# The projection of dt as one fp32 product in four 32-column groups, with the norm moved behind it

## The chip, the core and the metric

The kernel runs on one core of a Trainium2 chip. The metric is the device time of one execution in microseconds (us). Engines: PE is TensorE (its weight loads are listed apart as PEld), DVE is VectorE, ACT is ScalarE, POOL is GpSimd, SP issues the DMAs.

## The reference

Four layers run in sequence over x of 512 tokens by 1024 features: two of a first kind and two of a second. The change touches the first kind only, in its state-space branch. What matters of it:

```python
h = rmsnorm(x, attn_norm_g[layer])           # x * rsqrt(mean(x*x) + eps) * g
proj = h @ w_in[layer]
gm_u, gm_v, ssm_z, ssm_xbc, ssm_dt, da_q, da_k, da_v, gates = split_cols(proj, IN_SIZES)
...
dt = softplus(ssm_dt + dt_bias)              # ssm_dt: 16 columns of proj, one for each head
```

So `ssm_dt` is a product of h (512 x 1024) with 16 columns of `w_in`. The row factor rsqrt(...) depends on the token alone and the gain g on the feature alone, so that either can be applied before or after the product.

## The kernel before

Everything is fp32. Large products are split: each operand is written as a high part (fp32r) and a remainder, and TensorE makes three fp32r products (hi·hi, hi·lo, lo·hi) of 128 x 128 x 512 each, lines L571 to L573. x lies transposed in `x_t` (128 features by 8 tiles by 512 tokens). `h_hi` and `h_lo` hold the parts of h. Weights come in slabs of 128 x 1024 words into a ring of four (`w_raw`); ACT makes `w_hi` (L561), DVE `w_lo` (L566).

Results leave PE through four banks of PSUM, `pg`, taken in turn: the unit number modulo 4 is the bank. PE may begin a unit only when the bank's previous user has been read out (`bank_free`). In each layer of the first kind the units come in this order: four of `gv` (one for each 128 tokens `tt`), one of `dt`, then twelve of `xbc`, four at a time. With `gv` on banks 0, 1, 2, 3 the `dt` unit has bank 0, and the first four `xbc` units have banks 1, 2, 3, 0 (in the second layer all of this is turned by one bank; I name the banks as in the first). A slab of `xbc` contributes six products to each of the four units.

`gv` is computed on x that has its gain but not yet its norm, while the norm is being formed. Meanwhile DVE makes h (`h_val`, L809) from x, gain and the norm spread over all partitions (in the PSUM bank `spread1`), two tiles after each `gv` slab; ACT rounds it to `h_hi` (L802), POOL and DVE make `h_lo` (L555 and L813). ACT reads the four `gv` units out (L932).

dt: the 16 columns land in `dtw_raw`. ACT writes them twice as high part (L919) and DVE the remainder (L1412), 48 columns in all. PE makes 8 products of `h_hi` with all 48 columns (L2177) and 8 of `h_lo` with the first 16 (L2182), each waiting for its tile of h. They land in rows 0 to 15 and 32 to 47 of the bank. DVE reads the two out (L1430, L1431), which frees the bank, adds the bias (L1436), takes the maximum with 0 (L1437), and goes on with a softplus. All of it is program order on each engine; there is no scheduler.

Of the kernel before, what the change touches and what calls it, by code (L numbers as in the profile page):

```python
# [7 lines left out]
F32 = mybir.dt.float32  # L8
F32R = mybir.dt.float32r
ALU = mybir.AluOpType  # L10
ACT = mybir.ActivationFunctionType
AX = mybir.AxisListType

P = 128
# [4 lines left out]
KD = D // P  # L19
# [5 lines left out]
SSM_I, SSM_H, SSM_P, SSM_N, SSM_G, SSM_K = 1024, 16, 64, 128, 2, 4  # L25
# [6 lines left out]
C_DT = C_XBC + SSM_C  # L32
# [19 lines left out]
BANKS = 4  # L52
LO_DVE = [2, 5, 7]
# [60 lines left out]
def program(nc, t, out, depth=DEPTH, depth2=DEPTH):  # L114
    with ExitStack() as ctx:
# [3 lines left out]
        def over(name, offset, shape, dt):  # L119

            return nc.alloc_sbuf_tensor_at(name, shape, dt, offset=offset)
# [7 lines left out]
        def S(name):  # L129

            if name not in sems:
                sems[name] = ctx.enter_context(nc.semaphore(name))
            return sems[name]
# [6 lines left out]
        x_t = sb("x_t", [P, KD, SEQ])  # L140
# [4 lines left out]
        h_val = sb("h_val", [P, KD, SEQ])  # L145
# [17 lines left out]
        arena_at = next_place()  # L163
# [14 lines left out]
        def at(off, n, shape=None, **kw):  # L178
            a = arena[:, off:off + n]
            return a.rearrange(shape, **kw) if shape else a  # L180
# [5 lines left out]
        pg = ctx.enter_context(nc.psum_tensor("pg", [P, BANKS, SEQ], F32))  # L186
# [11 lines left out]
        dt_b, a_log, a_exp = cut(1), cut(1), cut(1)  # L198
# [49 lines left out]
        dt_t, dt_e, dt_z, dt_p, dt_1 = (at(18432 + 512 * i, 512)[0:SSM_H, :] for i in range(5))  # L248
# [18 lines left out]
        gstat = small[:, 0:8]  # L267
        lstat = small[:, 8:16]

        dtw = over("dtw", arena_at + 4 * 26624, [P, KD, 3 * SSM_H], F32R)  # L270
        dtw_raw = at(26624 + 3 * KD * SSM_H, KD * SSM_H, "p (k n) -> p k n", k=KD)

        m_val = at(0, 4096, "p (i s) -> p i s", i=KD)
        m_lo, m_hi = parts_at("m_lo", 0, KD), parts_at("m_hi", 14336, KD)
# [42 lines left out]
        SL, UN, PM = Schedule(), Schedule(), Schedule()  # L317
# [171 lines left out]
        def gate_unit(i):  # L489
# [5 lines left out]
        SWA_NORM = 3  # L495
        OUT_STEP = [1, 2, 3, 4, 5, 6, 7, 8]

        PER1 = {"par_landed": 16 * 15, "ffn_par_landed": 16 * 3, "dtw_landed": 16, "dtw_hi": 1, "dtw_lo": 1, "dt_done": 1, "h_val": KD, "h_hi_done": KD, "h_lo_dve": len(LO_DVE),
                "h_lo_pool": len(LO_POOL), "dt_x": 1, "dt_exp": 1, "a_exp_ready": 1, "conv_step": 36, "xs_ready": 3, "gv_ready": 1, "gm_rms": 1,
                "gm_vn": TT, "decay_in": 1, "decays": 1, "dt_ready": TT, "ac_split": 1, "gm_wt_ready": 1, "ya_ready": GM_G, "ya_hi_done": GM_G,  # L500
                "ya_split": GM_G, "ac_zeroed": 1, "cb_masked": SSM_G, "seg_bound": SSM_H, "seg_exp": SSM_H, "y_init": KD, "c_exp": SSM_H, "c_scaled": SSM_H, "decay_cb_even": PAIRS, "decay_cb_odd": PAIRS, "y_sq": KD, "y_sq_added": KD - 1, "xw_ready": SSM_G * (TT - 1), "y_gated": KD, "y_rms": 1, "y_inv": 1,
# [13 lines left out]
        def past(name):  # L515

            a, b = min(now[0], depth), max(now[0] - depth, 0)
            return a * PER1.get(name, 0) + b * PER2.get(name, 0)

# [14 lines left out]
        bank_free = [S(f"bank_free{i}") for i in range(BANKS)]  # L534
        pm_ready = S("pm_ready")
        pm_free = [S(f"pm_free{i}") for i in range(4)]

        def pmb(i):
            return pm[:, i % 4, :]
# [35 lines left out]
        def take_bank(pe, u, m, it):  # L575

            wait(pe, bank_free[u % BANKS], count(u // BANKS, m // BANKS, it))
            return pg[:, u % BANKS, :]
# [84 lines left out]
        def pm_left(eng, i):  # L663

            eng.wait_ge(pm_free[i % 4], i // 4 + 1)
# [32 lines left out]
        def gain(k):  # L698
            return g_norm[:, k, :]
# [104 lines left out]
        def norm_dve(dve, k, use, s, first, n, lows=LO_DVE):  # L804

            inv_b = pm_filled(dve, use)
            for i in range(first, first + n):
                dve.wait_ge(slab_done, s + i // 2 + 1)
                nc.vector.scalar_tensor_tensor(h_val[:, i, :], x_t[:, i, :], gain(k)[:, i:i + 1], inv_b, ALU.mult, ALU.mult).then_inc(S("h_val"), 1)  # L809
            for i in range(first + n):  # L810
                if i in lows and (i >= first or lows is not LO_DVE):
                    dve.wait_ge(S("h_hi_done"), past("h_hi_done") + i + 1)
                    nc.vector.tensor_tensor(h_lo[:, i, :], h_val[:, i, :], h_hi[:, i, :].bitcast(F32), ALU.subtract).then_inc(S("h_lo_dve"), 1)  # L813
            if first + n == KD:
                dve.wait_ge(S("h_val"), past("h_val") + KD)
                dve.sem_inc(pm_free[use % 4], 1)

        def norm_pool(pool):
            for i in LO_POOL:
# [3 lines left out]
        def tiles_ready(pe, of):  # L823

            def tile(k):
                for name, tiles in zip((of + "_lo_dve", of + "_lo_pool"), TILES[of]):
                    if k in tiles:
                        pe.wait_ge(S(name), past(name) + tiles.index(k) + 1)
            return tile
# [12 lines left out]
        def unit_left(eng, u, m=0, it=0):  # L842

            wait(eng, bank_free[u % BANKS], count(u // BANKS + 1, m // BANKS, it))
# [21 lines left out]
        def _(act):  # L866
            chain = Chain(act, "act_step")
# [46 lines left out]
            for l in range(depth):  # L914
                enter(l)
                if l > 0:
                    hi_ahead(SL["gv"])
                act.wait_ge(S("dtw_landed"), past("dtw_landed") + 16)
                nc.scalar.activation(dtw[:, :, 0:2 * SSM_H].rearrange("p k (b n) -> p k b n", b=2), dtw_raw.unsqueeze(2).broadcast_to([P, KD, 2, SSM_H]), ACT.Copy)\  # L919
                    .then_inc(S("dtw_hi"), 1)  # L920
                if l > 0:
                    norm_rows_act(act, PM["sums1"], PM["spread1"])
                hi_ahead(SL["gv"] + 1)
# [19 lines left out]
                hi_ahead(SL["xbc"])  # L943

                act.wait_ge(S("dt_x"), past("dt_x") + 1)
                chain(nc.scalar.activation(dt_e, dt_t, ACT.Abs))
                nc.scalar.activation(dt_e, dt_e, ACT.Exp, scale=-1.0).then_inc(S("dt_exp"), 1)
                nc.scalar.activation(a_exp[0:SSM_H, :], a_log[0:SSM_H, :], ACT.Exp).then_inc(S("a_exp_ready"), 1)

# [46 lines left out]
                for g in range(GM_G):  # L996
                    bank = unit_filled(act, SL["gu"] + g, UN["gu"] + g)
# [14 lines left out]
                for p in range(PAIRS):  # L1012
                    if p >= 2:
                        act.wait_ge(pm_ready, PM[("y", p - 2)] + 1)
                    for h in (2 * p, 2 * p + 1):
                        u = PM[("ac_row", p)] + h % 2
                        bank = pm_filled(act, u)
                        act.wait_ge(S("seg_bound"), past("seg_bound") + h + 1)
                        nc.scalar.activation(c_dec[h % 4], bank[:, P:SEQ], ACT.Exp).then_inc(S("c_exp"), 1)
                        for c in range(TT):  # L1020
                            done = nc.scalar.activation(seg[:, h % 4, c, :], seg[:, h % 4, c, :], ACT.Exp, bias=acneg[:, c, h:h + 1])
# [43 lines left out]
                for n in range(FILLS1):  # L1065
                    if n in PV1_AT:
                        h = PV1_AT.index(n)
                        u = PM[("pv", h)]
                        bank = pm_filled(act, u).rearrange("p (t n) -> p t n", t=TT)
                        chain(nc.scalar.activation(yt[:, h], bank, ACT.Copy))  # L1070
                        for tt in range(TT):
                            done = nc.scalar.activation(bank[:, tt, :], bank[:, tt, :], ACT.Square, accum_out=sub_sum[:, h, tt:tt + 1])
# [4 lines left out]
                    for k in (n - 2, n - 1) if n in W_AT else ():  # L1077
                        h, qi, u = k // TT, k % TT, PM[("w_t", k)]
                        if h >= 2:
                            act.wait_ge(pm_ready, PM[("pv", h - 2)] + 1)  # L1080
                        bank = pm_filled(act, u)
                        for kt in range(qi + 1):
                            done = nc.scalar.activation(wt(h, kt)[:, (qi - kt) * P:(qi - kt + 1) * P], bank[:, kt * P:(kt + 1) * P], ACT.Copy)
# [278 lines left out]
        def _(dve):  # L1362
            chain = Chain(dve, "dve_step")
# [43 lines left out]
            for l in range(depth):  # L1407
                enter(l)
                if l > 0:
                    lo_ahead(SL["gv"])  # L1410
                dve.wait_ge(S("dtw_hi"), past("dtw_hi") + 1)
                nc.vector.tensor_tensor(dtw[:, :, 2 * SSM_H:3 * SSM_H], dtw_raw, dtw[:, :, 0:SSM_H].bitcast(F32), ALU.subtract).then_inc(S("dtw_lo"), 1)  # L1412
                if l > 0:
                    norm_rows_dve(dve, chain, PM["sums1"], PM["spread1"])
                norm_dve(dve, l, PM["spread1"], SL["gv"], 0, 2)
# [11 lines left out]
                lo_ahead(SL["gv"] + 2)  # L1427
                lo_ahead(SL["gv"] + 3)
                dve.wait_ge(S("dt_done"), past("dt_done") + 1)
                chain(nc.vector.tensor_copy(dt_t, pg[0:SSM_H, UN["dt"] % BANKS, :]))  # L1430
                nc.vector.tensor_tensor(dt_t, dt_t, pg[2 * SSM_H:3 * SSM_H, UN["dt"] % BANKS, :], ALU.add).then_inc(bank_free[UN["dt"] % BANKS], 1)  # L1431
                unit_left(dve, UN["dt"])
                dve.wait_ge(S("par_landed"), past("par_landed") + 16 * 15)
                if l == 0:
                    dve.wait_ge(S("tables_landed"), 16)
                chain(nc.vector.tensor_scalar(dt_t, dt_t, dt_b[0:SSM_H, :], None, ALU.add))  # L1436
                nc.vector.tensor_scalar(dt_1, dt_t, 0.0, None, ALU.max).then_inc(S("dt_x"), 1)  # L1437

                def softplus_ratio():

# [683 lines left out]
        def _(pe):  # L2124
# [34 lines left out]
            for l in range(depth):  # L2159
# [9 lines left out]

                    slab_n(pe, SL["gv"], UN["gv"], hh, hl, 512, 4, 2, j, ready=x_parts(pe, l), between=between, late=l == 0 and j == 0)  # L2170

                pe.wait_ge(S("dtw_lo"), past("dtw_lo") + 1)
                bank, ready = take_bank(pe, UN["dt"], 0, 0), tiles_ready(pe, "h")
                def dt_high(k):

                    pe.wait_ge(S("h_hi_done"), past("h_hi_done") + k + 1)
                    return nc.tensor.matmul(bank[0:3 * SSM_H, :], dtw[:, k, :], hh(k), start=k == 0, stop=k == KD - 1)  # L2177

                def dt_low(k):

                    ready(k)
                    nc.tensor.matmul(bank[0:SSM_H, :], dtw[:, k, 0:SSM_H], hl(k), start=False, stop=False)  # L2182

                for k in range(6):
                    dt_high(k)
                for k in range(5):
                    dt_low(k)
                dt_high(6)
                for k in range(5, KD):
                    dt_low(k)  # L2190
                done = dt_high(7)
                done.then_inc(S("dt_done"), 1)

                for it in range(3):
                    for j in range(4):
                        slab_n(pe, SL["xbc"] + 4 * it, UN["xbc"] + 4 * it, hh, hl, 512, 4, 2, j, features=True)

                def xs_n(i):

# [373 lines left out]
        def _(sp):  # L2573
# [15 lines left out]
                sp.dma_start(x_in[:, :, part], t["x"][0, :, part].rearrange("(t p) c -> p t c", p=P)).then_inc(S(f"x_landed{q}"), 16)  # L2589

            def dt_load(l):
                sp.dma_start(dtw_raw, w_in[l, :, C_DT:C_DT + SSM_H].rearrange("(k p) n -> p k n", p=P), allow_slow_non_contiguous=True).then_inc(S("dtw_landed"), 16)

            def params_of(k):

# [163 lines left out]
```

## Time and profile before

| | |
|---|---|
| median of 3 runs | 2516.44 us (2516.0 to 2516.64) |
| profiled execution, span from first to last instruction | 2514.7 us |
| what lies around that span (median less span) | 1.7 us |
| PE busy in it | 2505.0 us |
| DVE, ACT, POOL busy | 1605.5, 1186.3, 317.8 us |

The profile lists no time of the profiled execution other than its span. Its products are pipelined, so that the time of one row (0.39 us) is longer than the distance between starts (0.23 us).

### The profile page before, as it was taken

To read this page: it belongs to the slowest core of one execution; us is meant where nothing else is said; L and a number is where in the kernel's file an instruction comes from. 1 tells how busy PE (TensorE), PEld (TensorE's weight loads), DVE (VectorE), ACT (ScalarE), POOL (GpSimd) and SP (SyncE) were. 2 spreads that over 40 slices of the span, in tenths; PEclk is the share of its full clock that TensorE was granted. 3 is DMA by queue.
4 is the path that set the end of the run, shared out by engine and by line. 5 is a ranking of instruction groups with operands and counts; after the bars stand their busy time and mean duration, and the time that the engine had idled before them with its cause. 6 is when DMAs were issued, how large, how long until landed. Compare 5 with 4: busy or idle time off the path is not lost.

```text
span 2514.7 us, 34027 instructions
## 1 busy us (share of the span) xinstructions
PE 2505.0 (100%) x12261; PEld 2048.5 (81%) x12261; DVE 1605.5 (64%) x2461; ACT 1186.3 (47%) x2185; POOL 317.8 (13%) x248
## 2 busy tenths in 40 slices
PE   9999999999999999999999999999999999999999
PEld 7887887888888887887877888888888777887777
DVE  6735767567777347538767567774355777647765
ACT  6534545544333235436354443333246555564563
POOL 1024201010111000225020101110020001210010
PEclk9999999999999999999999999999999999999999
DMA  6433342333333353452444333333324322332322
GB/s 143 95 83 66 87 92 75 65 112 93 100 92 98 97 112 88 88 80 71 92 81 69 96 92 100 92 99 96 99 79 108 86 62 62 91 93 76 84 59 76
DMA packets 400031, 221.94 MB, mean 88 GB/s; under 512 B 52736, under 2 KB 377376, under 8 KB 399648
## 3 DMA queue, kind: packets, MB, share of 16 engines
q1 hardware_dynamic: 399904, 220.26, 35.7%
q8 instruction: 79, 1.29, 0.2%
q14 instruction: 48, 0.39, 0.1%
HBM read 218.12 MB, written 2.10 MB: 88 GB/s over the span
## 4 chain that ended last, share of the span: by engine, by line
PE 96%; DVE 2%; ACT 1%; issue 1%; DMA 1%; SPq 0%; DVEq 0%
PE pg L571 29%; PE pg L572 28%; PE pg L573 28%; PE pm L671 3%; PE pm L2465 1%; PE pm L2349 1%; PE pm L2439 1%; PE pm L2314 1%; PE pm L2269 1%; DVE w_lo L566 1%; PE pm L2479 1%; PE pm L2506 1%; ACT w_hi L561 0%; PE pm L2272 0%; PE pm L2252 0%
## 5 line engine op out<-in xcount | busy, mean ns | idle before, releaser
L566 DVE TENSOR_TENSOR w_lo<-w_raw,w_hi 128x1024 fp32r<-128x1024 f32 (+3 forms) x440 | 538.8, 1226 | 516.3 <-ACT w_hi L561 514.4
L571 PE MATMUL pg<-h_hi,w_hi 128*128 128x512 f32 x1856 | 737.1, 397 | 0.3 <-ACT arena L1229 0.2
L573 PE MATMUL pg<-h_hi,w_lo 128*128 128x512 f32 x1856 | 723.3, 390 | 0.0
L572 PE MATMUL pg<-h_lo,w_hi 128*128 128x512 f32 x1856 | 723.1, 390 | 0.0
L561 ACT ACTIVATE w_hi<-w_raw 128x1024 fp32r<-128x1024 f32 (+3 forms) x440 | 434.1, 988 | 588.4 <-DMA w_raw<-in_w_in_dram 239.5
L571 PEld LDWEIGHTS pg<-h_hi,w_hi 128*128 128x128 f32 x1856 | 348.6, 188 | 77.6 <-issue 8.9
L573 PEld LDWEIGHTS pg<-h_hi,w_lo 128*128 128x128 f32 x1856 | 348.4, 188 | 73.4
L572 PEld LDWEIGHTS pg<-h_lo,w_hi 128*128 128x128 f32 x1856 | 348.9, 188 | 69.5 <-issue 1.4
L571 PE MATMUL pg<-w_hi,h_hi 128*128 128x512 f32 (+2 forms) x440 | 164.9, 375 | 0.0
L573 PE MATMUL pg<-w_hi,h_lo 128*128 128x512 f32 (+2 forms) x440 | 162.0, 368 | 0.0
L572 PE MATMUL pg<-w_lo,h_hi 128*128 128x512 f32 (+2 forms) x440 | 161.9, 368 | 0.0
L1743 DVE SCALAR_TENSOR_TENSOR arena<-conv_in,par,arena 128x512 f32<-128x512 f32 x176 | 131.9, 749 | 15.3 <-DVE arena L1743 11.0
L571 PE MATMUL pg<-f_hi,w_hi 128*128 128x512 f32 x352 | 136.9, 389 | 0.0
L572 PE MATMUL pg<-f_lo,w_hi 128*128 128x512 f32 x352 | 136.9, 389 | 0.0
L573 PE MATMUL pg<-f_hi,w_lo 128*128 128x512 f32 x352 | 136.9, 389 | 0.0
L1143 ACT ACTIVATE arena<-conv_in,par 128x512 f32<-128x512 f32 x88 | 71.9, 817 | 127.0 <-DVE conv_in L1737 127.0
L555 POOL TENSOR_TENSOR f_lo<-arena,f_hi x44 | 57.9, 1317 | 516.3 <-DVE f_hi L1751 516.3
L1737 DVE TENSOR_TENSOR conv_in<-pg,rinv 128x512 f32<-128x512 f32 x88 | 60.8, 691 | 80.7 <-PE pg L573 80.6
L571 PE MATMUL pg<-nb_parts,w_hi 128*128 128x512 f32 x256 | 101.9, 398 | 0.0
L573 PE MATMUL pg<-nb_parts,w_lo 128*128 128x512 f32 x256 | 99.7, 389 | 0.0
L571 PEld LDWEIGHTS pg<-w_hi,h_hi 128*128 128x128 f32 x440 | 82.8, 188 | 13.8 <-issue 1.9
L572 PEld LDWEIGHTS pg<-w_lo,h_hi 128*128 128x128 f32 x440 | 82.9, 188 | 12.9 <-issue 1.0
(417 smaller groups left out, 3753.2 us busy)
## 6 DMA issues: line engine op xcount, KB each, us to landing
w_raw<-in_w_in_dram SPq DMA_DIRECT2D x184, 512.0 KB, 4.7
w_raw<-in_ffn_w_up_dram SPq DMA_DIRECT2D x88, 512.0 KB, 3.7
w_raw<-in_w_out_dram SPq DMA_DIRECT2D x32, 512.0 KB, 3.6
w_raw<-in_ffn_w_down_dram SPq DMA_DIRECT2D x32, 512.0 KB, 3.6
w_raw<-in_w_branch_b_dram SPq DMA_DIRECT2D x16, 512.0 KB, 3.5
w_raw<-in_ffn_w_down_dram SPq DMA_DIRECT2D x16, 384.0 KB, 3.2
w_raw<-in_w_branch_a_dram SPq DMA_DIRECT2D x16, 256.0 KB, 2.9
w_raw<-in_w_branch_c_dram SPq DMA_DIRECT2D x16, 256.0 KB, 2.8
```

Of the source, the lines that this page charges most:

```text
L555: return nc.gpsimd.tensor_tensor(lo, value, hi.bitcast(F32), ALU.subtract)
L561: nc.scalar.activation(w_hi[:, s % HI, 0:n], w_raw[:, s % RAW, 0:n], ACT.Copy).then_inc(hi_done, 1)
L566: nc.vector.tensor_tensor(w_lo[:, s % RAW, 0:n], w_raw[:, s % RAW, 0:n], w_hi[:, s % HI, 0:n].bitcast(F32), ALU.subtract)\
L571: nc.tensor.matmul(dst, l_hi, r_hi, start=start, stop=False)
L572: nc.tensor.matmul(dst, l_hi, r_lo, start=False, stop=False)
L573: return nc.tensor.matmul(dst, l_lo, r_hi, start=False, stop=stop)
L671: done = nc.tensor.transpose(dst, src, ident[0:src.shape[0], 0:src.shape[0]])
L1143: nc.scalar.activation(facc[:, j, :], conv_in[:, j, 4:4 + SEQ], ACT.Identity, bias=fconv_b[:, bass.ds(i, 1)], scale=fconv_w[:, i, 2:3]).th ...
L1737: nc.vector.tensor_tensor(conv_in[:, j, 4:4 + SEQ], unit_filled(dve, SL["up"] + j, UN["up"] + j, 4, it), inv[:, :], ALU.mult)\
L1743: nc.vector.scalar_tensor_tensor(facc[:, j, :], conv_in[:, j, 4 - a:4 - a + SEQ], fconv_w[:, i, 2 - a:3 - a], facc[:, j, :], ALU.mult, ALU ...
L2269: done = nc.tensor.matmul(bank[rows, c * P:(c + 1) * P], xdt[:, c, h * 64:h * 64 + 64], seg[:, h % 4, c, :], start=True, stop=c == 0)
L2314: done = nc.tensor.matmul(bank[:, qi * P:(qi + 1) * P], wt(h, kt)[:, (qi - kt) * P:(qi - kt + 1) * P], qkv[:, kt, 1024 + h * P:1024 + (h + ...
```

## The change

The split of the dt weights goes, with ACT's and DVE's part in it. DVE multiplies the landed 16 columns by the gain instead. PE multiplies them with x itself in fp32, 8 products, product k into column group k % 4 of the array, so that four partial sums stand in rows 0, 32, 64 and 96 of the bank. DVE copies the first, adds the other three, and multiplies by the norm from `spread1`. The bias is added in the instruction that takes the maximum, and again as ACT's bias in the absolute value. PE's waits for the tiles of h move to the first four `xbc` slabs.

```diff
@@ arena @@
-        dtw = over("dtw", arena_at + 4 * 26624, [P, KD, 3 * SSM_H], F32R)
-        dtw_raw = at(26624 + 3 * KD * SSM_H, KD * SSM_H, "p (k n) -> p k n", k=KD)
+        dtw = at(26624, KD * SSM_H, "p (k n) -> p k n", k=KD)
+        DT_COLS = 4
@@ norm_dve @@
-                dve.sem_inc(pm_free[use % 4], 1)
+                if k >= depth:
+                    dve.sem_inc(pm_free[use % 4], 1)
@@ ACT @@
-                act.wait_ge(S("dtw_landed"), past("dtw_landed") + 16)
-                nc.scalar.activation(dtw[:, :, 0:2 * SSM_H]..., dtw_raw.unsqueeze(2).broadcast_to([P, KD, 2, SSM_H]), ACT.Copy)
...
-                chain(nc.scalar.activation(dt_e, dt_t, ACT.Abs))
+                chain(nc.scalar.activation(dt_e, dt_t, ACT.Abs, bias=dt_b[0:SSM_H, :]))
@@ DVE @@
-                dve.wait_ge(S("dtw_hi"), past("dtw_hi") + 1)
-                nc.vector.tensor_tensor(dtw[:, :, 2 * SSM_H:3 * SSM_H], dtw_raw, dtw[:, :, 0:SSM_H].bitcast(F32), ALU.subtract).then_inc(S("dtw_lo"), 1)
+                dve.wait_ge(S("dtw_landed"), past("dtw_landed") + 16)
+                nc.vector.tensor_tensor(dtw, dtw, gain(l).unsqueeze(2).broadcast_to([P, KD, SSM_H]), ALU.mult).then_inc(S("dtw_scaled"), 1)
...
                 dve.wait_ge(S("dt_done"), past("dt_done") + 1)
-                chain(nc.vector.tensor_copy(dt_t, pg[0:SSM_H, UN["dt"] % BANKS, :]))
-                nc.vector.tensor_tensor(dt_t, dt_t, pg[2 * SSM_H:3 * SSM_H, UN["dt"] % BANKS, :], ALU.add).then_inc(bank_free[UN["dt"] % BANKS], 1)
+                parts = [pg[32 * q:32 * q + SSM_H, UN["dt"] % BANKS, :] for q in range(DT_COLS)]
+                chain(nc.vector.tensor_copy(dt_t, parts[0]))
+                for q in range(1, DT_COLS):
+                    added = nc.vector.tensor_tensor(dt_t, dt_t, parts[q], ALU.add)
+                    if q < DT_COLS - 1:
+                        chain(added)
+                    else:
+                        added.then_inc(bank_free[UN["dt"] % BANKS], 1)
                 unit_left(dve, UN["dt"])
+                nc.vector.tensor_tensor(dt_t, dt_t, pmb(PM["spread1"])[0:SSM_H, :], ALU.mult).then_inc(pm_free[PM["spread1"] % 4], 1)
...
-                chain(nc.vector.tensor_scalar(dt_t, dt_t, dt_b[0:SSM_H, :], None, ALU.add))
-                nc.vector.tensor_scalar(dt_1, dt_t, 0.0, None, ALU.max).then_inc(S("dt_x"), 1)
+                nc.vector.tensor_scalar(dt_1, dt_t, dt_b[0:SSM_H, :], 0.0, ALU.add, ALU.max).then_inc(S("dt_x"), 1)
@@ PE @@
-                pe.wait_ge(S("dtw_lo"), past("dtw_lo") + 1)
-                (8 x dt_high, 8 x dt_low, each behind its tile of h)
+                pe.wait_ge(S("dtw_scaled"), past("dtw_scaled") + 1)
+                bank = take_bank(pe, UN["dt"], 0, 0)
+                for k in range(KD):
+                    q = k % DT_COLS
+                    done = nc.tensor.matmul(bank[32 * q:32 * q + SSM_H, :], dtw[:, k, :], x_t[:, k, :], start=k < DT_COLS, stop=k >= KD - DT_COLS)
                 done.then_inc(S("dt_done"), 1)
...
-                        slab_n(pe, SL["xbc"] + 4 * it, UN["xbc"] + 4 * it, hh, hl, 512, 4, 2, j, features=True)
+                        slab_n(pe, SL["xbc"] + 4 * it, UN["xbc"] + 4 * it, hh, hl, 512, 4, 2, j, features=True, ready=tiles_ready(pe, "h") if it == 0 else None)
```

PE before, from the first product of dt to the first product of the last unit in the first `xbc` slab (first layer; what stands in brackets is what the instruction waits for, `bank_free0` being bank 0):

```order
L2177 MATMUL pg<-h_hi,dtw 48x512 [waits h_hi_done,bank_free0,dtw_lo]
L2177 MATMUL pg<-h_hi,dtw 48x512 [waits h_hi_done] x5
L2182 MATMUL pg<-h_lo,dtw 16x512 [waits h_lo_pool] x2
...
L2182 MATMUL pg<-h_lo,dtw 16x512 [waits h_lo_dve]
L2177 MATMUL pg<-h_hi,dtw 48x512 [waits h_hi_done]
L571 MATMUL pg<-h_hi,w_hi 128x512 [waits bank_free1,split_done]
...
L571 MATMUL pg<-h_hi,w_hi 128x512 [waits bank_free2]
...
L571 MATMUL pg<-h_hi,w_hi 128x512 [waits bank_free3]
...
L571 MATMUL pg<-h_hi,w_hi 128x512 [waits bank_free0]
```

The same place of PE with the change:

```order
L2181 MATMUL pg<-x_t,arena 16x512 [waits bank_free0,dtw_scaled]
L2181 MATMUL pg<-x_t,arena 16x512 x7
L571 MATMUL pg<-h_hi,w_hi 128x512 [waits h_lo_pool,bank_free1,split_done]
...
L571 MATMUL pg<-h_hi,w_hi 128x512 [waits bank_free2]
...
L571 MATMUL pg<-h_hi,w_hi 128x512 [waits bank_free3]
...
L571 MATMUL pg<-h_hi,w_hi 128x512 [waits bank_free0]
```

The waits for h have left the dt products; the wait for bank 0, which dt itself fills, stands 18 products after dt in both.

DVE before, from the last two `w_lo` ahead of dt's read-out:

```order
L566 TENSOR_TENSOR w_lo<-w_raw,w_hi 128x1024 [waits h_val,hi_done]
L566 TENSOR_TENSOR w_lo<-w_raw,w_hi 128x1024 [waits hi_done]
L1430 COPY arena<-pg 16x512 [waits dt_done]
L1431 TENSOR_TENSOR arena<-arena,pg 16x512 [waits dve_step]
L1436 TENSOR_SCALAR arena<-arena,par 16x512 [waits tables_landed,par_landed,bank_free0]
L1437 TENSOR_SCALAR arena<-arena 16x512 [waits dve_step]
```

And with the change:

```order
L566 TENSOR_TENSOR w_lo<-w_raw,w_hi 128x1024 [waits hi_done,h_val]
L566 TENSOR_TENSOR w_lo<-w_raw,w_hi 128x1024 [waits hi_done]
L1429 COPY arena<-pg 16x512 [waits dt_done]
L1431 TENSOR_TENSOR arena<-arena,pg 16x512 [waits dve_step] x3
L1437 TENSOR_TENSOR arena<-arena,pm 16x512 [waits bank_free0]
L1442 TENSOR_SCALAR arena<-arena,par 16x512 [waits tables_landed,par_landed,pm_free1]
```

The read-out keeps its place behind the same two `w_lo`; bank 0 is released by the third addition instead of the first.

## Rows read from the trace of the kernel before

**Rows 1.** The page: span, busy time, granted clock in 40 slices.

```profile
span 2514.7 us, 34027 instructions
...
PE 2505.0 (100%) x12261; PEld 2048.5 (81%) x12261; DVE 1605.5 (64%) x2461; ACT 1186.3 (47%) x2185; POOL 317.8 (13%) x248
...
PEclk9999999999999999999999999999999999999999
```

**Rows 2.** Waits of PE: line waited for, us in total, times, longest.

```profile
PE pg L2568 <- DVE x_t L1953: 0.9, 1, 0.9
...
PE pg L2182 <- POOL h_lo L555: 0.6, 1, 0.6
```

**Rows 3.** Timeline of PE at dt, first layer: start, us, what, count.

```profile
37.10 1.56 PE L2177 MATMUL pg<-h_hi,dtw 128*48 128x512 f32 x6
...
40.91 0.95 PE L2182 MATMUL pg<-h_lo,dtw 128*16 128x512 f32 x2 [0.62 <-POOL h_lo L555]
...
41.93 0.39 PE L571 MATMUL pg<-h_hi,w_hi 128*128 128x512 f32 x1
...
46.03 0.39 PE L571 MATMUL pg<-h_hi,w_hi 128*128 128x512 f32 x1
```

**Rows 4.** Timeline of DVE around dt's read-out, first layer.

```profile
42.86 1.23 DVE L566 TENSOR_TENSOR w_lo<-w_raw,w_hi 128x1024 fp32r<-128x1024 f32 x1 [0.32 <-ACT w_hi L561]
44.01 0.67 DVE L1430 COPY arena<-pg 16x512 f32<-16x512 f32 x1
44.71 0.68 DVE L1431 TENSOR_TENSOR arena<-arena,pg 16x512 f32<-16x512 f32 x1
49.89 0.47 DVE L1436 TENSOR_SCALAR arena<-arena,par 16x512 f32<-16x512 f32 x1 [4.50 <-DMA c_pack<-in_c_pack_dram]
```

**Rows 5.** Timeline of PE at dt, second layer.

```profile
950.04 1.56 PE L2177 MATMUL pg<-h_hi,dtw 128*48 128x512 f32 x6
...
954.18 0.39 PE L571 MATMUL pg<-h_hi,w_hi 128*128 128x512 f32 x1
...
958.27 0.39 PE L571 MATMUL pg<-h_hi,w_hi 128*128 128x512 f32 x1
```

**Rows 6.** Timeline of DVE around dt's read-out, second layer.

```profile
956.60 0.67 DVE L1430 COPY arena<-pg 16x512 f32<-16x512 f32 x1
957.31 0.68 DVE L1431 TENSOR_TENSOR arena<-arena,pg 16x512 f32<-16x512 f32 x1
...
964.27 1.23 DVE L566 TENSOR_TENSOR w_lo<-w_raw,w_hi 128x1024 fp32r<-128x1024 f32 x1 [5.32 <-ACT w_hi L561]
```

**Rows 7.** Timeline of ACT: read-outs of gv, first layer, then second.

```profile
37.23 0.67 ACT L932 ACTIVATE arena<-pg,norm_inv 128x512 f32<-128x512 f32 x1
...
40.63 1.25 ACT L932 ACTIVATE arena<-pg,norm_inv 128x512 f32<-128x512 f32 x2
...
953.23 1.25 ACT L932 ACTIVATE arena<-pg,norm_inv 128x512 f32<-128x512 f32 x2
```

**Rows 8.** Timeline: fp32 products, full width, then in two 64-column groups.

```profile
934.18 1.02 PE L757 MATMUL pm<-rms,consts 128*128 128x512 f32 x2
...
1981.84 0.65 PE L2439 MATMUL pm<-arena 128*64 128x512 f32 x2
...
1982.32 0.60 PE L2439 MATMUL pm<-arena 128*64 128x512 f32 x2
...
1984.14 0.50 PE L571 MATMUL pg<-h_hi,w_hi 128*128 128x512 f32 x1
```

**Rows 9.** Timeline of PE's first products of 128 columns, and later ones.

```profile
3.66 1.97 PE L2145 MATMUL pm<-c_pack 128*128 128x128 f32 x8
...
7.39 4.38 PE L2145 MATMUL pm<-c_pack 128*128 128x128 f32 x28
...
12.54 1.04 PE L2139 MATMUL pm<-c_pack,arena 128*128 128x128 f32 x8
```

More of the change, by code:

```diff
@@ L496, in program @@
         OUT_STEP = [1, 2, 3, 4, 5, 6, 7, 8]
-        PER1 = {"par_landed": 16 * 15, "ffn_par_landed": 16 * 3, "dtw_landed": 16, "dtw_hi": 1, "dtw_lo": 1, "dt_done": 1, "h_val": KD, "h_hi_done": KD, "h_lo_dve": len(LO_DVE),
+        PER1 = {"par_landed": 16 * 15, "ffn_par_landed": 16 * 3, "dtw_landed": 16, "dtw_scaled": 1, "dt_done": 1, "h_val": KD, "h_hi_done": KD, "h_lo_dve": len(LO_DVE),
                 "h_lo_pool": len(LO_POOL), "dt_x": 1, "dt_exp": 1, "a_exp_ready": 1, "conv_step": 36, "xs_ready": 3, "gv_ready": 1, "gm_rms": 1,
@@ L917, in _ @@
                     hi_ahead(SL["gv"])
-                act.wait_ge(S("dtw_landed"), past("dtw_landed") + 16)
-                nc.scalar.activation(dtw[:, :, 0:2 * SSM_H].rearrange("p k (b n) -> p k b n", b=2), dtw_raw.unsqueeze(2).broadcast_to([P, KD, 2, SSM_H]), ACT.Copy)\
-                    .then_inc(S("dtw_hi"), 1)
                 if l > 0:
@@ L1429, in _ @@
                 dve.wait_ge(S("dt_done"), past("dt_done") + 1)
-                chain(nc.vector.tensor_copy(dt_t, pg[0:SSM_H, UN["dt"] % BANKS, :]))
-                nc.vector.tensor_tensor(dt_t, dt_t, pg[2 * SSM_H:3 * SSM_H, UN["dt"] % BANKS, :], ALU.add).then_inc(bank_free[UN["dt"] % BANKS], 1)
+                parts = [pg[32 * q:32 * q + SSM_H, UN["dt"] % BANKS, :] for q in range(DT_COLS)]
[6 more added lines that the diff above has]
+                        added.then_inc(bank_free[UN["dt"] % BANKS], 1)
                 unit_left(dve, UN["dt"])
+                nc.vector.tensor_tensor(dt_t, dt_t, pmb(PM["spread1"])[0:SSM_H, :], ALU.mult).then_inc(pm_free[PM["spread1"] % 4], 1)
+                pm_left(dve, PM["spread1"])
                 dve.wait_ge(S("par_landed"), past("par_landed") + 16 * 15)
@@ L2170, in _ @@
                     slab_n(pe, SL["gv"], UN["gv"], hh, hl, 512, 4, 2, j, ready=x_parts(pe, l), between=between, late=l == 0 and j == 0)
-                pe.wait_ge(S("dtw_lo"), past("dtw_lo") + 1)
[L2173 to L2191, printed above, removed]
+                pe.wait_ge(S("dtw_scaled"), past("dtw_scaled") + 1)
[3 more added lines that the diff above has]
+                    done = nc.tensor.matmul(bank[32 * q:32 * q + SSM_H, :], dtw[:, k, :], x_t[:, k, :], start=k < DT_COLS, stop=k >= KD - DT_COLS)
                 done.then_inc(S("dt_done"), 1)
@@ L2591, in dt_load @@
             def dt_load(l):
-                sp.dma_start(dtw_raw, w_in[l, :, C_DT:C_DT + SSM_H].rearrange("(k p) n -> p k n", p=P), allow_slow_non_contiguous=True).then_inc(S("dtw_landed"), 16)
+                sp.dma_start(dtw, w_in[l, :, C_DT:C_DT + SSM_H].rearrange("(k p) n -> p k n", p=P), allow_slow_non_contiguous=True).then_inc(S("dtw_landed"), 16)
             def params_of(k):
```

## Prediction

> **What bounds the kernel now.** I read the page first: PE is busy for 2505.0 of 2514.7 us, at a granted clock of 1.00 (2.4 GHz) in all 40 slices [rows 1]. Then the waits of PE: once it works, its longest single wait is 0.9 us, and one of 0.6 us is at dt, for a tile of `h_lo` [rows 2]. So a microsecond taken off PE's stream is a microsecond off the time, and any wait of PE counts in full, unless it ends something that would have been waited for anyway. The reader is therefore to follow PE alone through the dt stage, and the others only where PE will wait for them. The third view is the timeline of that stage on PE, DVE and ACT, in both layers of the first kind.
>
> **What PE does there now.** In the first layer dt begins at 37.10 and the first `xbc` product at 41.93: 4.83 us [rows 3]. In the second it is 950.04 to 954.18: 4.14 us [rows 5]. The pitch of products is (958.27 - 954.18) / 18 = 0.227 us [rows 5], so 16 products are 3.64 us, and the rest (1.2 and 0.5 us) is waiting for tiles of h. From `xbc`'s first product PE runs 18 products (units on banks 1, 2, 3) and then takes bank 0, which dt has filled: at 46.03 in the first layer, at 958.27 in the second [rows 3, 5]. DVE had released that bank at 44.71 + 0.68 = 45.39 and 957.31 + 0.68 = 957.99 [rows 4, 6]. The wait for bank 0 is thus not in the trace, but it was missed by only 0.64 and 0.28 us. That is the place to watch.
>
> **The new dt products.** An fp32 product of 512 columns shows as two records; a full-width one took 1.02 us for its two, of which I count 0.85 us as PE's time, since one record lasts 0.16 us longer than its distance to the next (0.39 against 0.227) [rows 8, 3]. Eight in a row are 8 x 0.85 = 6.8 us. Do column groups run together? In the second block's products of 64 columns, two records start at 1981.84 and the next two at 1982.32, 0.48 later; the whole set of 16 records (columns 512, 384, 256 and 128, twice each, two groups) is over at 1984.14, in 2.30 us [rows 8]. One after another those would be 2 x 1280 columns x 0.85/512 = 4.25 us. So two groups do run together. I take four groups to do it too: two rounds of 0.85, 1.7 us. Bounds: 1.7 us, and 6.8 us if four groups don't overlap at all. I take 1.8 with the change of shape (a first 128-wide record after it lasted 0.50 instead of 0.39, so 0.1 us [rows 8]). By itself this frees 4.83 - 1.8 = 3.0 us and 4.14 - 1.8 = 2.3 us: 5.3 us in all.
>
> **What DVE does with it.** DVE comes to the read-out only after the `w_lo` that starts at 42.86 and waits for ACT [rows 4]. None of what stands before the read-out on ACT and DVE depends on dt: it hangs on the last `gv` slab, which has ended before dt begins. So the copy still starts at 44.01 and at 956.60 [rows 4, 6], however early PE is. Then come three additions for one. The distance from copy to addition is 0.70 and 0.71 us. Release of bank 0, first layer: 44.01 + 3 x 0.70 + 0.68 = 46.79; second: 956.60 + 3 x 0.71 + 0.68 = 959.41.
>
> **The sum.** PE would come to bank 0 at 37.10 + 1.8 + 18 x 0.227 = 43.0 in the first layer, and still a little later since the bank of the second unit is released only halfway through ACT's two read-outs at 40.63, about 41.3 (0.9 to 1.1 us of wait, then it works until about 44.1) [rows 7]. It waits there until 46.79 + 0.05. Before, it began at 46.03: +0.8 us. Second layer: bank of the second unit at about 953.9, arrival at about 956.7, released 959.41 + 0.05 against 958.27: +1.2 us. A restart out of a wait costs a first record of 0.50 instead of 0.39, 0.1 us each [rows 8]. Sum: 0.9 + 1.3 = **+2.2 us**. PE's whole gain turns into a wait, of about 2.7 us in each layer at bank 0 and 0.7 to 1.1 us before it, and the two extra additions are what is left over.
>
> The length of dt drops out of this sum: with release at 46.84 and 959.46, dt may take 46.84 - 37.10 - 4.09 = 5.6 us or 959.46 - 950.04 - 4.09 = 5.3 us before it counts.
>
> **Edits at nothing.** ACT's 8 x 32-column copy and one DVE operation of 16 columns go or are replaced by one of the same shape, ahead of waits on PE. The multiplication by the norm and the merged bias: DVE has 4.5 us of idle time in the first layer before L1436 (it waits for the tables) [rows 4] and 5.3 us in the second before its next `w_lo` [rows 6]; the added three operations are about 2.1 us less a 0.47 us one. Uncovered they would be 1.6 us of DVE, still before a `w_lo` that PE needs two slabs later. The PSUM bank of the norm is held some microseconds longer; its next user is the transposition of the xs, far later. The waits on h that move to `xbc`: the first slab needs tiles 0 and 1 only, and the last tile of POOL was there by 40.91 [rows 3]. POOL's clearing of the buffer that dt's weights lay in waits for dt's end and comes a little earlier; nobody waits for it there. Nothing is issued to SP in another order. A later PE delays the loads behind it by as much as itself.
>
> The profile's span becomes 2514.7 + 2.2 = 2516.9; the median lies 1.7 us above the span before, and I keep that: 2516.44 + 2.2 = **2518.6 us**.
>
> **Rivals.** *One: the four groups don't run together.* dt is then 6.8 us. PE reaches bank 0 at 37.10 + 6.8 + 4.1 = 48.0 and 961.0, later than the release: +2.0 and +2.7, sum +4.7, 2521.1 us. It decides from a length of 5.3 us on; the pairs in [rows 8] speak against it, four groups and 16 columns are not in the trace. In TensorE: Matmul & The Clock Gate (Part 3) the Trainium skill says that a weight load overlaps products in flight only when the row group differs, and here all eight have the same rows; by that rule the sum would be this rival's and more. The trace disagrees for two groups, whose records start in pairs. 8%.
>
> *Two: the clock falls.* At the start of the program, after idling, eight products of 128 columns took 1.97 us, at 12.54 eight took 1.04 [rows 9]: half rate, 1.2 GHz. Pitch there (1.04 - 0.16) / 8 = 0.11; the 44 records from 3.66 to 7.39 + 4.38 = 11.77 at that pitch are 5.0 us instead of 8.1, so one fall costs up to 3.1 us. PE will stand still for about 2.7 us, three times its longest wait now [rows 2]. If it falls in both layers: 2.2 + 6.2 = +8.4, 2524.8 us; in one, +5.3, 2521.7. For: no row shows the clock after so long a wait in mid-program. Against: PE works for 1.4 and 2.7 us on either side of the shorter wait, and at 0.9 us nothing falls. The Trainium skill states in the same page (Part 1) that the array's clock is halved by idling and given back by work; the trace's start agrees. Both layers 5%, one 7%.
>
> *Three, on the other side: the bank is free in time.* If the read-out came early enough, all 5.3 us would stay: 2511.1 us. This decides where DVE would release bank 0 by 43.0 instead of 46.8; its program order behind the `w_lo` of 42.86 speaks against. 4%. In between lies a release some tenths earlier than I have it, up to nothing lost: that is within my own case.
>
> *My own case*, bank 0 binds and dt's length does not matter: 76%, range +1.0 to +3.6 (additions and restart 0.3 to 0.7 off in each layer), 2517.4 to 2520.0.
>
> **How the numbers follow.** 0.2% is 5.0 us, about what a measurement tells from no change. Within it: my case and the first rival (76 + 8), a one-layer fall about at the edge is counted slower. Faster by more than 0.2% only the third rival: 4%. Slower: 7 + 5 = 12%. Chances 0.04, 0.84, 0.12. The range goes from 2516.5 (nothing lost) to 2521.8 (columns one after another, or one fall of the clock); it leaves out the third rival and the double fall.
>
> **What the profile would show.** Right: 16 records of dt's product (two for each), over within 2 us; the first product on the second `xbc` unit waiting for ACT; the first product on the fourth waiting for DVE's third addition (2.5 to 3 us); the copy on DVE at 44.0 and 956.6 as before; granted clock 1.00 behind it. Wrong: dt's records in single file to about 44; a clock below 1.00 behind the wait; DVE's copy earlier or much later than before, which would void the sum; or a new wait of PE on `w_lo` later in `xbc`.

## The result and the profile after

The changed kernel takes 2520.27 us (median of 21 runs, 2518.24 to 2522.29); the kernel before takes 2516.03 us (21 runs, 2515.7 to 2517.01). The ratio is 1.0017, 95% interval 1.001 to 1.0023: slower by 4.2 us, less than 0.2%. The forecast was 2518.6 us, 2516.5 to 2521.8. The profiled execution has a span of 2518.7 us, 4.0 us more than before [rows 1].

The waits of PE after the change, us in total, times, longest:

```profile
PE pg L571 <- DVE arena L1431: 5.0, 2, 2.5
...
PE pg L571 <- ACT arena L930: 1.0, 2, 0.7
PE pg L2558 <- DVE x_t L1958: 0.8, 1, 0.8
```

The wait for a tile of h at dt [rows 2] is gone. In its place stand two waits of 2.5 us for the last addition of the read-out, and two shorter ones for ACT's read-out of gv. The timeline of PE in the first layer, start, us, what, count:

```profile
37.17 1.91 PE L2181 MATMUL pg<-x_t,arena 128*16 128x512 f32 x16
39.01 0.50 PE L571 MATMUL pg<-h_hi,w_hi 128*128 128x512 f32 x1
39.34 0.40 PE L572 MATMUL pg<-h_lo,w_hi 128*128 128x512 f32 x1
...
41.34 0.50 PE L571 MATMUL pg<-h_hi,w_hi 128*128 128x512 f32 x1 [0.67 <-ACT arena L930]
...
46.87 0.50 PE L571 MATMUL pg<-h_hi,w_hi 128*128 128x512 f32 x1 [2.51 <-DVE arena L1431]
47.21 0.39 PE L572 MATMUL pg<-h_lo,w_hi 128*128 128x512 f32 x1
47.44 0.40 PE L573 MATMUL pg<-h_hi,w_lo 128*128 128x512 f32 x1
```

`xbc` begins at 39.01 instead of 41.93, and yet the unit on bank 0 begins at 46.87 instead of 46.03 [rows 3]. DVE in the same place:

```profile
42.85 1.23 DVE L566 TENSOR_TENSOR w_lo<-w_raw,w_hi 128x1024 fp32r<-128x1024 f32 x1 [0.30 <-ACT w_hi L561]
43.99 0.67 DVE L1429 COPY arena<-pg 16x512 f32<-16x512 f32 x1
44.70 2.12 DVE L1431 TENSOR_TENSOR arena<-arena,pg 16x512 f32<-16x512 f32 x3
46.85 0.68 DVE L1437 TENSOR_TENSOR arena<-arena,pm 16x512 f32<-16x512 f32 x1
```

The copy stands where it stood (44.01 before, [rows 4]); the three additions end at 46.82, and PE starts 0.05 us later. In the second layer all of it comes 1.05 us later than before (the copy at 957.65 instead of 956.60 [rows 6]), so the first layer cost 1.05 us. There the third addition ends at 960.48:

```profile
957.65 0.67 DVE L1429 COPY arena<-pg 16x512 f32<-16x512 f32 x1
958.36 2.12 DVE L1431 TENSOR_TENSOR arena<-arena,pg 16x512 f32<-16x512 f32 x3
```

PE there:

```profile
951.18 1.91 PE L2181 MATMUL pg<-x_t,arena 128*16 128x512 f32 x16
953.02 0.50 PE L571 MATMUL pg<-h_hi,w_hi 128*128 128x512 f32 x1
...
960.53 0.79 PE L571 MATMUL pg<-h_hi,w_hi 128*128 128x512 f32 x1 [2.52 <-DVE arena L1431]
961.12 0.63 PE L572 MATMUL pg<-h_lo,w_hi 128*128 128x512 f32 x1
961.55 0.63 PE L573 MATMUL pg<-h_hi,w_lo 128*128 128x512 f32 x1
...
963.68 0.50 PE L572 MATMUL pg<-h_lo,w_hi 128*128 128x512 f32 x1
964.02 0.40 PE L573 MATMUL pg<-h_hi,w_lo 128*128 128x512 f32 x1
964.26 0.40 PE L571 MATMUL pg<-h_hi,w_hi 128*128 128x512 f32 x1
```

Look at the distance between starts: 0.43 us behind the wait, 0.23 from 964 on. The windows of the same stretch (us, busy us of PE, PEld, DVE, ACT and POOL, granted clock, DMA share, GB/s) show why:

```profile
951.00:953.00 2.00, 2.00 (x18) 0.36 (x16) 1.41 (x2) 0.84 (x2) 0.15 (x1) 1.00 0.15 32
960.60:962.00 1.40, 1.40 (x4) 1.11 (x5) 1.06 (x2) 1.34 (x5) 0.00 (x0) 0.50 0.00 0
964.00:968.00 4.00, 4.00 (x19) 3.26 (x18) 1.23 (x1) 3.88 (x7) 0.00 (x0) 1.00 0.69 124
```

The clock is granted at half, 1.2 GHz, behind the second layer's wait, and reads 1.00 again from 964.0 on. The first layer's wait is as long (2.51 us), and the products behind it keep their 0.23 us: a wait of this length does not bring the fall each time. The page doesn't show the fall at all. Its clock row is 40 nines as before, since a 9 stands for 90% or more of a slice of 63 us; it takes the windows or the mean. The tenth product behind the wait starts at 964.26; at full pace it would be 960.53 + 0.34 + 8 x 0.227 = 962.69, so this fall cost 1.6 us. The bill of this execution: 1.05 (first layer) + 960.53 - (958.27 + 1.05) = 1.21 (second) + 0.1 (restart) + 1.6 (clock) = 4.0 us, the whole difference of the spans.

The other executions fit this, as far as their times and mean clocks tell; no trace of them is on record. Their times, by the mean granted clock listed with each (the 21 runs of the changed kernel):

```
clock 1.000   1 run    2518.24
clock 0.999  13 runs   2519.20 to 2520.66
clock 0.998   7 runs   2520.93 to 2522.29
```

The mean is taken over the whole span and listed to three digits, so it says that the clock fell, not where. In the profiled execution it holds this fall and the last 1.7 us of the program, which read 0.50 too, with no instruction left on any engine and nothing lost. The one run at 1.000 is 2.2 us above the median of before. The 21 runs of before lie within 1.3 us of each other; its profiled execution is at 1.000, and so are its 64 further runs beside the experiments.

### The profile page after: what moved, and what is told of

The parts are those of the page before. It is cut to its first block, busy times and chain, and to the rows that moved or that the text cites. A ratio compares the mean times of both kernels' runs of the same rounds, so it can differ in the third digit from the quotient of the medians.

```text
span 2518.7 us, 34037 instructions
## 1 busy us (share of the span) xinstructions
PE 2503.0 (99%) x12261; PEld 2045.3 (81%) x12261; DVE 1609.2 (64%) x2465; ACT 1185.3 (47%) x2183; POOL 316.1 (13%) x248
## 4 chain that ended last, share of the span: by engine, by line
PE 96%; DVE 2%; ACT 1%; issue 1%; DMA 1%; SPq 0%; ACTq 0%; DVEq 0%
PE pg L571 29%; PE pg L573 28%; PE pg L572 28%; PE pm L671 3%; PE pm L2455 1%; PE pm L2339 1%; PE pm L2429 1%; PE pm L2304 1%; DVE w_lo L566 1%; PE pm L2259 1%; ACT w_hi L561 1%; PE pm L2469 1%; PE pm L2496 1%; PE pm L2262 0%; PE pm L2242 0%
```

## Experiments

My theory after the result: bank 0, released late by DVE, costs 2.2 us whatever the length of dt, and the clock that falls behind PE's wait costs the rest. Rivals: the fp32 products or the read-out themselves are too dear; the products in column groups disturb the clock; something later in the kernel. "Before" in a comparison is the kernel before the change on the same chip (2516.55 us for the first four, 2515.94 us for the last four). All differences here are a few us, and the interval of a ratio is about 0.0009, or 2.3 us, on either side. Three ratios are clear of 1: one column group and the late read-out are slower, four groups with the spare bank faster. The other five are not told from no change, and what is said of them rests on the trace and on how little the runs of one kernel differ. What is called faster or slower than the change as made compares the distances of the two kernels from their own before.

**Fillers in the wait.**

```diff
+                def fillers(tt):
+                    if tt == 3:
+                        spare = take_pm(pe, PM["dt_n"])
+                        for _ in range(18):
+                            nc.tensor.transpose(spare[:, 0:P], ident, ident)
...
-    slab_n(..., ready=tiles_ready(pe, "h") if it == 0 else None)
+    slab_n(..., ready=tiles_ready(pe, "h") if it == 0 else None, between=fillers if (it, j) == (0, 0) else None)
```

> The changed kernel with 18 additional products of 128 columns (identity by identity, into a bank of PSUM that nobody reads before it is overwritten) put between the third and the fourth unit of the first xbc slab, where PE waits 2.5 us for bank 0. At 0.11 us each they are 2.0 us and end inside the wait. My theory: the 4.2 us of the changed kernel are 2.2 us of waiting longer for bank 0 and about 2 us of a clock that falls in some executions behind that wait; with the fillers the clock stays, so the median is 2518.2 us and the spread of the runs is that of before (about 1 us instead of 4). Rival: the 2 us beyond the wait for the bank come from something else (a later stage); then the median stays at 2520.3 us and the spread at 4 us.

Measured: 2518.69 us (2518.12 to 2519.43, 11 runs), ratio 1.0008 (0.9999 to 1.0017); the clock is 1.000 in all runs. PE in the second layer:

```profile
957.41 2.13 PE L2189 MATMUL pm<-c_pack 128*128 128x128 f32 x18
960.08 0.50 PE L571 MATMUL pg<-h_hi,w_hi 128*128 128x512 f32 x1 [0.54 <-DVE arena L1431]
960.41 0.40 PE L572 MATMUL pg<-h_lo,w_hi 128*128 128x512 f32 x1
```

The unit on bank 0 starts no earlier for the fillers: it still waits for L1431. But the products behind it keep their pace of 0.23 us, the spread is 1.3 us instead of 4, and what is left is +2.1 us, the price of the bank alone. Work that nobody needs takes 2.1 us off the changed kernel's +4.2. That is the clock's share; nothing is left over for a later stage.

**Two column groups**, inside the ring of banks.

```diff
-        DT_COLS = 4
+        DT_COLS = 2
```

> The changed kernel with 2 column groups instead of 4: DVE has one addition as before the change, PE's 8 fp32 products are 4 rounds of two. My theory (bank 0 binds, pairs overlap, 3.5 us of dt): release at 45.4 in the first layer against 46.03 before, 0.28 us before its time in the second, 0.1 us restart each: 0.7 us faster than before, 2515.3 us, no clock fall since PE waits under 1 us. Rival (groups don't overlap, dt 6.8 us): 4.7 us slower than before, 2520.7 us.

Measured: 2515.85 us, ratio 0.9997 (0.9988 to 1.0006), 0.7 us below before: as expected in size, and not told from no change by the interval. The clock is 1.000 in all 11 runs. The trace shows how it comes about:

```profile
36.94 3.61 PE L2181 MATMUL pg<-x_t,arena 128*16 128x512 f32 x16
40.48 0.50 PE L571 MATMUL pg<-h_hi,w_hi 128*128 128x512 f32 x1
...
45.18 0.50 PE L571 MATMUL pg<-h_hi,w_hi 128*128 128x512 f32 x1 [0.32 <-DVE arena L1431]
```

PE begins the unit on bank 0 at 45.18, with four groups at 46.87, before the change at 46.03. dt is 1.7 us longer than with four groups, and the kernel is 4.9 us faster: the length of dt did not count. The two additions less did, by some 2.9 us of earlier release and by the 2 us of clock that no longer fall.

**One column group.** No addition, the copy releases the bank.

```diff
-        DT_COLS = 4
+        DT_COLS = 1
...
-                chain(nc.vector.tensor_copy(dt_t, parts[0]))
+                nc.vector.tensor_copy(dt_t, parts[0]).then_inc(bank_free[UN["dt"] % BANKS], 1)
```

> The changed kernel with a single column group: 8 fp32 products one after another, and DVE's read-out is the copy alone. My theory: dt is 6.8 us, PE reaches bank 0 at 48.0 and 961.0 where it was 46.03 and 958.3, the bank is free by then, no wait: 4.7 us slower than before, 2520.7 us, with the narrow spread of before. Rival (a single small group is cheaper than a full-width fp32 product): below 2518 us.

Measured: 2521.71 us (2521.2 to 2522.34, all at 1.000), ratio 1.002 (1.0011 to 1.0029), +5.2 us. In its trace:

```profile
37.13 7.04 PE L2181 MATMUL pg<-x_t,arena 128*16 128x512 f32 x16
44.10 0.50 PE L571 MATMUL pg<-h_hi,w_hi 128*128 128x512 f32 x1
```

7.04 us for the eight, without a wait behind them: this is the price of fp32 products in single file, and it is above the 5.3 us from which dt's length counts. The 0.5 us beyond the forecast are covered by dt itself, 6.97 us from its start to the next product instead of 6.8, and the changes of shape before and behind it, 0.1 us each, in each layer.

**dt out of the ring of banks.** Its unit goes to a bank of the other ring (`pm`), which is idle then; same products, same DVE operations.

```diff
-("gv", 4, 4), ("dt", 0, 1),
+("gv", 4, 4),
-("spread1", 1), ("dt_n", 1)
+("spread1", 1), ("dt", 1), ("dt_n", 1)
...
-                bank = take_bank(pe, UN["dt"], 0, 0)
+                bank = take_pm(pe, PM["dt"])
...
-                parts = [pg[32 * q:32 * q + SSM_H, UN["dt"] % BANKS, :] for q in range(DT_COLS)]
+                dt_bank = pm_filled(dve, PM["dt"])
+                parts = [dt_bank[32 * q:32 * q + SSM_H, :] for q in range(DT_COLS)]
```

> The changed kernel with dt's unit taken out of the ring of four pg banks and put into a bank of the other ring (pm), which is idle at this time; all products and DVE operations as in the changed kernel. xbc's fourth unit then takes the bank that the fourth gv unit has left. My theory: no wait of 2.5 us, the whole saving of dt's products appears: 5.3 us faster than before, 2510.7 us, spread as before. Rival (the products themselves or DVE's longer read-out cost the time, not the bank): no faster than before.

Measured: 2511.6 us (2510.73 to 2512.11), ratio 0.998 (0.997 to 0.9989): 4.9 us faster than before, 9 us faster than the change as made. It is the fastest version of all. PE in the first layer:

```profile
37.38 1.91 PE L2181 MATMUL pm<-x_t,arena 128*16 128x512 f32 x16
39.22 0.50 PE L571 MATMUL pg<-h_hi,w_hi 128*128 128x512 f32 x1
...
43.23 0.39 PE L573 MATMUL pg<-h_hi,w_lo 128*128 128x512 f32 x1
43.45 0.39 PE L571 MATMUL pg<-h_hi,w_hi 128*128 128x512 f32 x1
43.68 0.39 PE L572 MATMUL pg<-h_lo,w_hi 128*128 128x512 f32 x1
```

From 39.22 on PE never stops: the fourth unit begins at 43.45, 2.6 us before its old time. The short waits for ACT are gone too, because without dt's unit each `xbc` unit follows the `gv` unit of its own number. The clock is 1.000 in all 11 runs, with the same fp32 products in four column groups as in the change: these products alone do not make it fall.

**The same spare bank without the change**, as a control: the same edit made to the kernel before.

> The kernel before the change (split weights, 16 products behind the tiles of h), with dt's unit in a bank of the other ring. My theory: bank 0 was never waited for there (0.64 and 0.28 us in hand), so the spare bank alone is worth nothing: within 0.5 us of before. Rival (the spare bank is a gain of its own, by a cheaper order of banks, and the fp32 product adds nothing to it): about 5 us faster than before, as the changed kernel with the spare bank was.

Measured: 2515.57 us, ratio 0.9998 (0.9989 to 1.0007), 0.4 us below before. By itself the bank is worth nothing that can be told from no change; the gain of 4.9 us needs both.

**An earlier read-out.** Bank 0 stays dt's.

```diff
                 lo_ahead(SL["gv"] + 2)
+                (wait for dt, copy, three additions)
                 lo_ahead(SL["gv"] + 3)
-                (wait for dt, copy, three additions)
```

> The changed kernel with DVE's copy and three additions put one w_lo earlier (between the last two that stood ahead of them). My theory: bank 0 is released at about 45.3 in the first layer (46.03 was when PE began it before the change) and about 0.8 us before its old time in the second, restarts cost 0.1 us each: 1.2 us faster than before, 2515.3 us on this chip's 2516.5, and no clock fall, since PE waits 1.3 us or less. Rival (DVE's read-out is not what PE waits for): no change against the changed kernel, 4 us slower than before.

Measured: 2514.56 us (2514.2 to 2515.18), ratio 0.9995 (0.9986 to 1.0004), 1.4 us below before and about 5.6 us below the change as made. DVE:

```profile
40.73 1.21 DVE L566 TENSOR_TENSOR w_lo<-w_raw,w_hi 128x1024 fp32r<-128x1024 f32 x1
41.86 0.67 DVE L1428 COPY arena<-pg 16x512 f32<-16x512 f32 x1
42.57 2.12 DVE L1430 TENSOR_TENSOR arena<-arena,pg 16x512 f32<-16x512 f32 x3
44.61 1.21 DVE L566 TENSOR_TENSOR w_lo<-w_raw,w_hi 128x1024 fp32r<-128x1024 f32 x1
```

Only the order on DVE differs. PE's longest wait for the read-out is 1.0 us, and the clock is 1.000 in all runs.

**A late read-out in the kernel before.**

```diff
+                for _ in range(4):
+                    chain(nc.vector.tensor_copy(dt_e, pg[0:SSM_H, UN["dt"] % BANKS, :]))
                 chain(nc.vector.tensor_copy(dt_t, pg[0:SSM_H, UN["dt"] % BANKS, :]))
```

> The kernel before the change with four more copies of the same shape (16 x 512 out of the bank) ahead of dt's read-out, so that bank 0 is released 2.8 us later and PE waits 2.2 us in the first layer and 2.5 us in the second; PE's own products are those of before. My theory (the clock falls behind such a wait, whatever the products were): 4.7 us of waiting and 0.2 us of restarts, and on top about 2 us of fallen clock in some executions: median about 2522.5 to 2523.5 us with a spread of 3 to 4 us. Rival (the clock falls because of the fp32 products in column groups ahead of the wait): 2521.4 us with the narrow spread of before.

Measured: 2522.45 us (9 runs), ratio 1.0025 (1.0015 to 1.0035). The runs form two clusters: four at 2521.35 to 2521.73 and five at 2522.45 to 2522.99, four of these five with a clock of 0.999. Its waits:

```profile
PE pg L571 <- DVE arena L1433: 4.6, 2, 2.5
```

The waits are 2.10 and 2.46 us long. The kept trace is of a run of the lower cluster, at 1.000, so where the clock fell in the upper one is not seen. Its place behind these waits is concluded from the mean clock, below 1.000 in four of nine runs here and in none of the 31 runs of before beside them. So the clock can fall without any fp32 product or column group ahead of the wait; the rival's narrow time is only the lower cluster, 5.4 to 5.8 us above before (the spans of the two kept traces differ by 5.1). But my spread of 3 to 4 us was wrong: it is 1.6 us, and the fall is rarer and, by the distance of the clusters, costs 1.2 us. Two things differ from the changed kernel: the first wait is 2.10 instead of 2.51 us, and the further short wait (0.67 and 0.32 us) some 3 us ahead of each long one is missing. Whether either makes the difference was not tried.

**Two groups and the spare bank.** The edit of the spare bank, with `DT_COLS = 2`.

> The changed kernel with the spare bank, and two column groups instead of four. My theory: with the wait for bank 0 gone the length of dt counts again, 3.61 instead of 1.91 us in each layer: 3.4 us slower than with four groups and a spare bank, so 1.5 us faster than before, where inside the ring two groups were 4.4 us faster than four. Rival (the length of dt does not count here either): as four groups with a spare bank, 4.9 us faster than before.

Measured: 2514.23 us (2513.47 to 2515.01), ratio 0.9993 (0.9984 to 1.0002), 1.7 us below before, where four groups were 4.9 us below: 3.2 us of gain lost, against 3.4 forecast. The intervals of the two ratios touch (0.9984 to 1.0002 and 0.997 to 0.9989), so this rests on the lengths of dt, 3.61 and 1.91 us in the traces, and on runs that don't overlap. Outside the ring four groups beat two; inside it two beat four. It is the wait that turns the sign.

## Why the prediction was right, point by point

**PE's saving.** Forecast 1.8 us for the new dt, measured 1.91 us for its records and 0.1 us of a change of shape before it (37.17 where 37.08 would follow). `xbc` starts at 39.01 where I had 38.9. Four groups do run together: 7.04, 3.61 and 1.91 us with one, two and four. The first rival (8%) did not happen, and its price of +4.7 us came out as +5.2.

**The bank.** Release forecast 46.79, measured 44.70 + 2.12 = 46.82. Forecast +0.9 and +1.3 us, measured 1.05 and 1.3. The waits came out a little shorter than forecast, 2.5 us instead of 2.7 at bank 0, and 0.67 and 0.32 us instead of 0.7 to 1.1 at the second unit, which changes nothing: what counts is the release. The spare bank, the earlier read-out and the two groups each remove or shorten this wait by another way, and each gave what the sum said, within 0.4 us. The one run with a mean clock of 1.000 is +2.2 us, and the kernel with fillers +2.1: this is the forecast of my own case.

**The third rival** (bank free in time, 2511.1 us) did not happen in the change, for the reason given, DVE's order. Its price was right: built on purpose it measured 2511.6 us beside a before of 2516.55, 4.9 us of the 5.3.

**The clock: the chance and the size were wrong, the mechanism right.** What happened is my own case (76%) with the second rival (12%) on top of it, and the measured median lies above the 2520.0 us at which my own case ended. The prediction's own sign of being wrong, a clock below 1.00 behind the wait, came. I held against the rival that the clock stayed at waits of 0.9 us, and that PE works on both sides of the shorter wait; neither says anything of 2.5 us, and the mean clock was below 1.000 in 20 of 21 runs. The term that the sum put at nothing is 2.0 us in the median (2520.27 - 2518.24), and the forecast's time was 1.7 us low. That 2516.0 + 2.2 + 2.0 gives the measured time again proves nothing, since the 2.0 is taken from it; the fillers are the independent measure, and they took off 2.1.

The size of a fall was wrong the other way. I took 3.1 us from the slow products at the start of the program [rows 9], a stretch of 8.1 us in which the profile reads a granted clock of 1.00 all the same, so that only their pace speaks for the half clock. In mid-program a fall cost 1.6 us.

So the range held in part by luck. By the rival's prices even one fall stood at 2521.7 us, counted as slower than before by more than 0.2%, and two at 2524.8, outside the range. The falls came much oftener than I thought and cost half: the two errors offset each other, and the median stayed inside the range and, at +4.2 us, below 0.2%.

**The edits at nothing.** Nothing of them shows in PE's waits. DVE's chain still waits 1.7 us for the tables in the first layer. ACT's rows stand within 0.1 us of where they stood (1.05 us later in the second layer, up to the fall of the clock), and POOL's clearing comes 1.4 us earlier in the first, as forecast.

## What to carry to other kernels

On an engine that is busy all the time, a shorter stage is worth its time only until the next buffer that it takes; look who frees it and how near before was to waiting (here 0.64 and 0.28 us). If a faster product leaves more partial sums, the read-out holds the bank longer: give it a buffer outside the ring, or read it out earlier, before cutting the products. And price a new wait of TensorE with the clock that may fall behind it; a spread that grows from 1 to 4 us is its mark, and a mean clock in the third digit, not the page's 40 slices.

## What the runs showed of the hardware

fp32 products of 512 columns in one, two and four column groups took 7.04, 3.61 and 1.91 us for eight: the overlap is nearly complete even with the same 128 rows, 16 columns of weights each. The Trainium skill (TensorE: Matmul & The Clock Gate, Part 3) has a measured speedup of 2.38 times for three column tiles of 32; the trace agrees that column groups run together, with 3.7 times for four.

The granted clock fell to half behind a wait of 2.5 us in the one trace that shows it; there PE had stood still from 958.0 to 960.5, and the clock read 1.00 again after eight products. In the same trace an equal wait brought no fall. The mean clock was below 1.000 in 20 of 21 runs of this kernel and in four of nine of the one with the late read-out. It was 1.000 in all 77 runs of the seven other kernels of the experiments, whose waits on other engines, once PE works, are 1.0 us or less.

Eighteen transposes of 128 columns in the wait kept it at 1.000 in 11 of 11. The start of the program points the same way: from 3.66 to 11.52 us PE of the kernel before runs nothing but transposes, and a window of one microsecond holds 5 of them at 7.4 us and 12 at 10.4 us. The Trainium skill says in TensorE: Matmul & The Clock Gate (Part 4) that transposes don't count as work for the clock in the same way as products; the runs here disagree.
